# Rows of y turned beside the output products instead of inside the last dense head, in a two-layer hybrid encoder on one core

## What is computed

```python
def mixer_layer(x, w_in, w_out, ...):
    h = x @ w_in                                   # split into heads A, B, C
    ya = window_gqa(...) * silu(ga)                # 256 columns
    ob = diff_attention(qb, kb, vb, lam, valid)    # 4 dense heads of 128 columns
    yb = rms_norm(ob, subln_w) * (1 - lam_init) * silu(gb)
    yc = rms_norm(y_f + y_b, c_norm_w) * silu(gc)  # 256 columns
    y = concatenate([ya, yb, yc], axis=-1)
    return y @ w_out

h = layer_norm(ALPHA * h + mixer_layer(h, ...), g, b)      # twice
```

## Time and profile before

| what | value |
|---|---|
| median of 3 runs | 1952.11 us (1952.1 to 1958.83) |
| the profiled execution, its own time | 1951.07 us |
| its span, first to last instruction | 1949.8 us |
| TensorE matmuls busy | 1741.2 us, 89% |
| VectorE busy | 1143.0 us, 59% |
| ScalarE busy | 886.3 us, 45% |
| GpSimd busy | 405.2 us, 21% |
| mean granted clock of TensorE | 0.966 of full |

### The profile page before, as it was taken

One profiled execution on the slowest core, in us unless ns is written; L12 is line 12 of the kernel. 1 busy time (PEld: TensorE's weight loads), 2 busy tenths in 40 slices (PEclk: granted clock), 3 DMA queues, 4 the chain that ended last, 5 costly groups with the idle time before them and its releaser, 6 DMA issues. The chain is left out here.

```text
span 1949.8 us, 37518 instructions
## 1 busy us (share of the span) xinstructions
PE 1741.2 (89%) x14474; PEld 1621.5 (83%) x14474; DVE 1143.0 (59%) x2793; ACT 886.3 (45%) x2700; POOL 405.2 (21%) x390
## 2 busy tenths in 40 slices
PE   3899999999889998978999989999998898988796
PEld 3798998999788787857988989989998787876696
DVE  6475584345457777874175845833554576767615
ACT  4434544345425665663053444452452354656603
POOL 5430221210121001020454203113103001012044
PEclk9899999999989999999999999999998899999998
DMA  7200100100110000032122001011001000003312
GB/s 248 63 26 12 55 23 27 51 25 10 34 45 6 28 10 28 17 130 94 44 95 70 23 12 55 23 32 46 28 10 52 23 9 28 30 8 106 111 62 87
DMA packets 98192, 91.89 MB, mean 47 GB/s; under 512 B 6176, under 2 KB 88336, under 8 KB 98016
## 3 DMA queue, kind: packets, MB, share of 16 engines
q1 hardware_dynamic: 98016, 89.49, 14.1%
HBM read 68.30 MB, written 21.17 MB: 46 GB/s over the span
## 5 line engine op out<-in xcount | busy, mean ns | idle before, releaser
L798 PE MATMUL psum<-w_hi,hT_hi 128*128 128x256 f32 x2400 | 704.0, 293 | 24.3 <-DVE rb L1687 13.7
L798 PE MATMUL psum<-w_hi,hT_lo 128*128 128x256 f32 x2400 | 681.8, 284 | 0.0
L798 PE MATMUL psum<-w_lo,hT_hi 128*128 128x256 f32 x2400 | 681.3, 284 | 0.0
L798 PEld LDWEIGHTS psum<-w_hi,hT_hi 128*128 128x128 f32 x2400 | 459.8, 192 | 36.0 <-DVE rb L1687 16.7
L798 PEld LDWEIGHTS psum<-w_hi,hT_lo 128*128 128x128 f32 x2400 | 459.7, 192 | 0.0
L798 PEld LDWEIGHTS psum<-w_lo,hT_hi 128*128 128x128 f32 x2400 | 459.1, 191 | 0.0
L760 POOL CAST w_hi<-w_raw 128x512 fp32r<-128x512 f32 (+1 forms) x168 | 110.2, 656 | 1377.7 <-DMA w_raw<-in_w_in 813.2
L764 POOL TENSOR_TENSOR w_lo<-w_raw,w_hi 128x512 fp32r<-128x512 f32 (+1 forms) x168 | 211.7, 1260 | 30.9 <-DVE neg_max L1827 19.4
L1826 DVE TENSOR_REDUCE row_max<-psum 128x1 f32<-128x1024 f32 x136 | 165.4, 1216 | 33.7 <-PE psum L938 33.5
L1087 PE MATMUL psum<-vg_b,aT_b 128*128 128x128 f32 (+1 forms) x1224 | 159.4, 283 | 23.3 <-ACT aT_b L1387 23.3
L1087 PEld LDWEIGHTS psum<-vg_b,aT_b 128*128 128x128 f32 (+1 forms) x1224 | 145.3, 189 | 32.2 <-ACT aT_b L1387 28.6
(11 more groups left out here) (161 smaller groups left out, 2677.8 us busy)
## 6 DMA issues: line engine op xcount, KB each, us to landing
w_raw<-in_w_in SPq DMA_DIRECT2D x104, 256.0 KB, 3.7
h_dram<-hbuf SPq DMA_DIRECT2D x16, 512.0 KB, 2.6
w_raw<-in_w_out SPq DMA_DIRECT2D x16, 512.0 KB, 4.1
hbuf<-h_dram SPq DMA_DIRECT2D x16, 512.0 KB, 5.5
qk_b<-y_dram SPq DMA_DIRECT2D x16, 512.0 KB, 3.3
y_dram<-y_stage SPq DMA_DIRECT2D x96, 64.0 KB, 1.6
w_raw<-in_w_in SPq DMA_DIRECT2D x12, 512.0 KB, 4.5
hbuf<-in_x SPq DMA_DIRECT2D x8, 512.0 KB, 7.3
```

Source lines behind the costliest of these rows:

```text
L798: last = nc.tensor.matmul(out_ap, lhs[a](k), rhs[b](k), start=k == 0 and a + b == 0, stop=k == KT - 1 and b == 1)
```

## The change

Inside pass B3 nothing of y is transposed, copied or subtracted any more. `output` begins with the transposes of y tiles 0, 1 and 2, and each unit of the first column chunk is followed by the transposes of the tile three further on, until all are done. ScalarE's and VectorE's parts move along. `y_load` has room for four tiles; tiles 0 to 3 are loaded in pass B3 as before, and the loads of tiles 4 and on come behind the loads of the last `hbuf` tiles and of the two layer norm vectors in the queue, each after the transposes of the tile four before.

```diff
-Y_LAG = 3
+Y_AHEAD = 3
+Y_BUFS = 4
...
-    y_load = ...[:, 0:2 * DM].rearrange("p (s c) -> p s c", s=2)
+    y_load = ...[:, 0:Y_BUFS * DM].rearrange("p (s c) -> p s c", s=Y_BUFS)
...
 # load_y
-            if t >= 2:
-                wait_filled(sp, ("y", l, t - 2, 1))
+            if t >= Y_BUFS:
+                wait_filled(sp, ("y", l, t - Y_BUFS, 1))
...
 # SyncE's queue, in the last head
             for t in range(n):
                 save_y(l, "B3", t)
-                load_y(l, t)
+                if t < Y_BUFS:
+                    load_y(l, t)
             load_h(l, range(6, n))
             load_ln(ln_g[l], ln_b[l])
+            for t in range(Y_BUFS, n):
+                load_y(l, t)
             load_chunk(l, "O", 2)
...
 # TensorE, end of a step of pass_b
-                if not nx and t >= Y_LAG:
-                    transpose_y(l, t - Y_LAG)
...
 # TensorE, output
-            late = {0: n - 3, 1: n - 2, 3: n - 1}
+            for t in range(Y_AHEAD):
+                transpose_y(l, t)
             for c in range(DM // CW):
                 for x in units(l, "O", c):
                     project(l, "O", c, x)
-                    if c == 0 and x in late:
-                        transpose_y(l, late[x])
+                    if c == 0 and x + Y_AHEAD < n:
+                        transpose_y(l, x + Y_AHEAD)
...
 # ScalarE, end of a step of pass_b
-                if not nx and t >= Y_LAG:
-                    hi_of_rows("y", l, t - Y_LAG)
...
 # ScalarE, behind the pass
-            for t in range(n - Y_LAG, n):
+            for t in range(n):
                 hi_of_rows("y", l, t)
...
 # VectorE, end of a step of pass_b
-                if not nx and t >= Y_LAG:
-                    lo_of_rows("y", l, t - Y_LAG)
...
 # VectorE, output
-            late = {0: n - 3, 1: n - 2, 3: n - 1}
+            for t in range(Y_AHEAD):
+                lo_of_rows("y", l, t)
...
-                    if c == 0 and t in late:
-                        lo_of_rows("y", l, late[t])
+                    if c == 0 and t + Y_AHEAD < n:
+                        lo_of_rows("y", l, t + Y_AHEAD)
```

More of the change, by code:

```diff
@@ L310, in bank_plan @@
                         add(("meta", l, nx, c), 6 + c)
-                if not nx and t >= Y_LAG:
-                    transposed("y", l, t - Y_LAG, (7, 6))
-        for t in range(n - Y_LAG, n):
+        for t in range(Y_AHEAD):
             transposed("y", l, t, (7, 6))
@@ L317, in bank_plan @@
                 add(("unit", l, "O", c, t), t % 2)
+                if c == 0 and t + Y_AHEAD < n:
+                    transposed("y", l, t + Y_AHEAD, (7, 6))
         if l < DEPTH - 1:
@@ L504, in build @@
     sB.close()
-    y_load = qk_b[:, 1].bitcast(F32).rearrange("p s t -> p (s t)")[:, 0:2 * DM].rearrange("p (s c) -> p s c", s=2)
+    y_load = qk_b[:, 1].bitcast(F32).rearrange("p s t -> p (s t)")[:, 0:Y_BUFS * DM].rearrange("p (s c) -> p s c", s=Y_BUFS)
     psum = top.enter_context(nc.psum_tensor("psum", [P, 8, 512], F32))
@@ L520, in build @@
     ln_in = sem("ln_in")
-    y_in = [sem(f"y_in{i}") for i in range(2)]
+    y_in = [sem(f"y_in{i}") for i in range(Y_BUFS)]
     y_saved = [sem(f"y_saved{i}") for i in range(Y_SLOTS)]
@@ L662, in load_y @@
                 sp.wait_ge(y_saved[s], 16 * sum(1 for k in range(1, n + 1) if k % Y_SLOTS == s))
-            if t >= 2:
-                wait_filled(sp, ("y", l, t - 2, 1))
-            sp.dma_start(y_load[0:rows(t), t % 2], y_dram[t, 0:rows(t)]).then_inc(y_in[t % 2], 16)
+            if t >= Y_BUFS:
+                wait_filled(sp, ("y", l, t - Y_BUFS, 1))
+            i = t % Y_BUFS
+            sp.dma_start(y_load[0:rows(t), i], y_dram[t, 0:rows(t)]).then_inc(y_in[i], 16)
         sp.dma_start(lam_sb[:], b_lam.partition_broadcast(P)).then_inc(setup_in, 16)
@@ L834, in transpose_y @@
         def transpose_y(l, t):
-            pe.wait_ge(y_in[t % 2], 16 * (sum((q_tiles(m) + 1 - t % 2) // 2 for m in range(l)) + t // 2 + 1))
-            transpose_rows("y", l, t, y_load[:, t % 2])
+            i = t % Y_BUFS
+            pe.wait_ge(y_in[i], 16 * (sum(len(range(i, q_tiles(m), Y_BUFS)) for m in range(l)) + t // Y_BUFS + 1))
+            transpose_rows("y", l, t, y_load[:, i])
         def transpose_rows(what, l, t, src):
```

## The result

| | before | changed |
|---|---|---|
| median | 1952.11 us | 1961.72 us |
| lowest and highest of 14 runs | 1948.18 to 1958.83 us | 1955.17 to 1968.5 us |
| profiled execution, its span | 1949.8 us | 1964.8 us |
| mean granted clock in it | 0.966 | 0.957 |

The ratio is 1.0048 with a 95% interval of 1.0037 to 1.0058, that is 7 to 11 us more. The forecast was 1957.5 us in a range from 1948 to 1964: no change or a little more. The time lies in the range, on the side that was named, 4 us above the forecast.

The account below looks back on a forecast made before the run. The prediction took a VectorE-ScalarE loop to bound the last head and TensorE the output stage. Terms -8.3 + 8.8 + 4.3 + 0.5 + 0.9 = +6.2 us gave 1957.5 us, range 1948 to 1964.

Parts of the forecast that it names:

- Part 1: Last dense head: seven steps lose the y subtraction and fall to 7.33 us each, 8.3 us less.
- Part 2: Last combine to first output product: three y tiles pass through two banks, 8.8 us more over both layers.
- t0: Start of the first y transposes after the last values: T + 7.07 in layer 0, T + 5.48 in layer 1.
- T: Time of the last head's last combine: 890.52 in layer 0, 1832.79 in layer 1 in the kernel before.
- Part 3: First output chunk: 5 more y tiles transposed between units on TensorE at 0.87 us each, 4.3 us more.
- Part 4: First output chunk: y tile 4, queued behind other loads, arrives just in time; 0, or up to 2 us each layer.
- Rival D: First output chunk: y tile 4 is late, 1 to 2 us in each layer, 1960 us; chance 0.10.
- Part 5: TensorE's clock falls after layer 1's head step 3, 0.5 us more, and in layer 0's first products, 0.9 us more.
- A: Between head and output, the transpose chain drops TensorE's clock in both layers: +12.0 us, 1963 us; chance 0.14.
- B: End of layer 0's head: the clock holds, last values take 2.0 us; +1.5 us, 1952.6 us; chance 0.14.
- C: Last head: the clock falls in all seven steps, which take 7.82 us; +9.7 us, 1961 us; chance 0.10.
- E: Whole kernel: a gain, from a seam at old length with faster values and transposes, -6.8 us, 1944 us; chance 0.04.

Follow-up runs that it names:

- x6_loop: The kernel before, with VectorE's y subtraction moved behind the maxima in the last head, and third probabilities and values output given other banks; 1939.51 us.
- x7_all: The changed kernel with the edits of x1_loads, x2_banks and x3_norm together; 1956.7 us.
- x4_warm: The changed kernel with 18 idle transposes of the identity on TensorE in the last step of the last head; 1956.01 us.
- x11_changed: The changed kernel itself measured once more, for a second trace; 1962.89 us.
- x3_norm: The changed kernel with ScalarE's copy of y tile 0 put ahead of the last norm of the last head; 1965.37 us.
- x1_loads: The changed kernel with loads of y tiles 4 and on put ahead of the last hbuf tiles and layer norm vectors; 1954.95 us.
- x2_banks: The changed kernel with the first three y tiles transposed into six banks instead of two; 1963.12 us.

## Why the prediction was right, and where it was off

- **Part 1, the steps (-8.3, measured -7.2 with the fall of the clock in one step).** Right: 7.32 us a step, as worked out from one clean step. The fall that was expected behind step 3 of layer 1 came, 7.84 us (1816.61 to 1824.45). In layer 0 and in layer 1 one of the steps drawn out by GpSimd became 0.4 us longer (8.22 us), which I had put at 0; such steps come and go in all kernels alike (8.23 us in layer 1 of x6_loop, 7.81 us in x7_all), so I count it as no term of the change.
- **Part 2, the seam (+8.8, measured +9.3).** The chain at full clock was right to a tenth: "The first product starts at t0 + 5.9", measured 5.82 and 5.98. Its start t0 was off in both layers. In layer 1 I had T + 5.48 and it was T + 8.02. The step that failed is that the last `values` of layer 1 run at full clock as before, which stood in t0 without a word: I took the clock of the old seam over to the new one, though the transposes of y ahead of the last step were part of what kept it. x4_warm shows it: with TensorE at work in that gap t0 is T + 5.50. In layer 0 I had the half clock through the whole chain, t0 at T + 7.07 and the product at T + 14.3; the clock came back as the chain began, t0 was T + 6.35 and the product T + 12.2. One error was 2.5 us, the other -2.1 us, and that they nearly cancel is luck. In the second trace (x11_changed) t0 of layer 0 was T + 7.17, as predicted, the product T + 13.0, and the whole seam term +10.2.
- **Part 3, the chunk (+4.3).** Right: 3.71 us between units with a tile and 2.84 us without, and 4.3 us in the kernels that don't wait for a load.
- **Part 4, the loads (0, measured +2.3).** This is the largest miss of a term. The tile was wanted at t0 + 12.4 and its transposes began at t0 + 14.7 in layer 0. The sum failed at "the last of their traffic ran until about 1854.4, 7.6 us", a figure of layer 1 that stood for both layers. In layer 1 it nearly fits: the second norm vector landed at t0 + 10.6 and y tile 4 at t0 + 11.9, where the sum had 10.1 and 11.4. In layer 0 the five loads took 9.8 us from the first issue to the last landing, and y tile 4 landed 2.4 us behind them, not 1.3. The sum gave each load the whole way until it had landed, and those behind took a part of it. Why this costs more in layer 0 is open. In the second trace the wait was 0.9 us. Rival D, "1 to 2 us in each layer", came in one layer.
- **Part 5, the clock (+0.5 and +0.9).** The first came. The second did not: the products started at full clock. The rule of the Trainium skill ("TensorE: Matmul & The Clock Gate", "A second HAM failure mode: psum-queue depth-cycling") would have had the clock fall in the chain of transposes with its gaps. In the changed kernel it did not: 1.00 from 899 to 905 and from 1848 to 1854 us, with gaps of 1.5 to 1.8 and of 1.0 us. In x3_norm, with a gap of 2.91 us, it did (0.51 from 898 to 902 us).
- **The rivals.** A is out as it was told, since the clock held through the chain; a loss of about its price for the products of one layer (2.5 us) came in layer 1 ahead of the chain. B is out: the last `values` of layer 0 took 3.53 and 4.02 us in the two traces, not 2.0. C is out, since the steps ran at 7.33 us. E, the gain, is out for this change, as the seam grew; but the gain that it speaks of can be had, for x6_loop gets the head's 7 us without a longer seam.

The sum by terms was +6.2; the trace has +8.8, the timed runs +9.6. The forecast held by the sign and by a wide range; of its size a third was missing. What is open: about 3 us of x1_loads's gain, and which part of the spread between runs of one kernel (1955 to 1968 us) comes from the clock. Over the 14 runs of the changed kernel the time falls as the mean granted clock rises (correlation -0.90; 1955.17 us at 0.968, 1966.08 us at 0.957). That points to the clock, but no experiment tests what moves it. Much of the spread lies outside the compared stretches, where the programs are the same: the thirteen traces of this record take 825 to 836 us up to the second `combine` of layer 0's last head, and 762 to 767 us from the last addition of layer 0's output to the second `combine` of layer 1's last head.

## What to carry to other kernels

Work that stands in a loop's longest path costs nearly its whole length (1.19 of 1.28 us here), and moving it to another stage is only one way to get rid of it: first look on the same engine, in the same loop, for the place where it waits, here 2.06 us for 1.28 us of work. Such a move needs the buffers too, since what the moved instruction releases is released later. And when work is taken from an engine whose clock follows its activity, or a load is put behind others, price the place that lost its cover: in x2_banks and x4_warm the shorter seam met the late load at once.

## What the runs showed of the hardware

- TensorE's granted clock fell to 0.50 after a stretch in which it worked 1.28 of 4 us, and 18 transposes without any use (2.1 us) in that stretch kept it at 1.00. The last `values` took 2.25 us instead of 4.05 for it (x4_warm, layer 1).
- A load of 512 KB took 3.3 us from issue to landing (median of 16, the kernel before), and 10.5 us (median) for three that were issued within 1.5 us behind 2 MB of others on the same queue. They landed in the order of the queue, but the ones behind took a part of the bandwidth: 2.7 MB had moved when the first 2.2 MB had landed.
- Two traces of programs that are the same up to a point may differ there by 5.6 us, at a granted clock of 0.83 against 0.91 in one stretch of 100 us.
